# Two-block kernel: raw transposes of x with the norms applied at evacuation, and two reordered transitions

## The reference, cut to what matters

```python
h = concat([meta, x])                      # 1040 x 1024
u = rmsnorm(h, norm_g)                     # h * rsqrt(mean(h^2) + eps) * norm_g
f_in, f_gate, q, k, v, a_gate = split(u @ w_in)
f_out = (real(fftn(f_in, positions and channels)) @ w_fmix + b_fmix) * silu(f_gate)
a_out = gqa_attention(rope(rmsnorm(q)), rope(rmsnorm(k)), v) * silu(a_gate)
x = rmsnorm(h + concat([f_out, a_out]) @ w_out, final_g)[meta:]
# second block
p = rmsnorm(x, norm_mix_pre) @ w_in_2      # q, k, v, three convolution parts, two gates
merged = sigmoid(g_att) * (stick_breaking(q, k, v) @ w_att) + sigmoid(g_conv) * (conv(...) @ w_conv)
x = x + rmsnorm(merged @ w_out_2, norm_mix_post)
x = x + rmsnorm((gelu(conv(g)) * conv(a)) @ w_down, norm_ffn_post)   # g, a from rmsnorm(x, norm_ffn_pre) @ w_up
```

## Time and profile before

| What | Value |
|---|---|
| Median of 3 runs | 2228.54 us (2226.97 to 2229.95) |
| Profiled execution | 2228.94 us, span of its profile 2227.1 us |
| Mean granted TensorE clock | 0.981 of full speed |
| TensorE matmuls, share of the span | 2118.0 us, 95% |
| VectorE | 1115.5 us, 50% |
| ScalarE | 838.9 us, 38% |
| POOL | 745.9 us, 33% |

### The profile page before, as it was taken

How to read it: one execution, slowest core, us unless ns; L and a number is a source line. 1 busy time by engine, 2 the same in 40 slices (tenths; PEclk the granted TensorE clock), 3 DMA queues, 4 the chain that set the end, 5 groups by cost and what they waited for, 6 DMA issues and landing times.

```text
span 2227.1 us, 27859 instructions
## 1 busy us (share of the span) xinstructions
PE 2118.0 (95%) x10545; PEld 1747.8 (78%) x10545; DVE 1115.5 (50%) x1608; ACT 838.9 (38%) x1485; POOL 745.9 (33%) x661
## 2 busy tenths in 40 slices
PE   5899999999988999999999999989999999999996
PEld 4687888999767788787877888868888888878785
DVE  7347658888253376767657652442222222221523
ACT  5133228999232364554546421331221222111212
POOL 3222142222331322222222343233333333367672
PEclk7999999999999999999999999999999999999998
DMA  5031120010241211111212543421111111132432
GB/s 172 24 122 52 52 95 30 11 49 11 67 134 57 65 62 51 54 59 52 70 48 80 170 139 108 132 76 48 47 47 47 47 47 47 48 112 94 148 107 76
DMA packets 142923, 164.69 MB, mean 74 GB/s; under 512 B 7091, under 2 KB 108999, under 8 KB 142823
## 3 DMA queue, kind: packets, MB, share of 16 engines
q1 hardware_dynamic: 118663, 98.10, 14.4%
q10 hardware_dynamic: 24160, 65.23, 8.4%
HBM read 133.94 MB, written 29.36 MB: 73 GB/s over the span
## 4 chain that ended last, share of the span: by engine, by line
PE 84%; DVE 9%; ACT 3%; issue 2%; DMA 1%; ACTq 0%; POOL 0%; DVEq 0%
PE psum L667 18%; PE psum L669 18%; PE psum L668 18%; PE psum L989 15%; PE psum L885 3%; PE psum L897 3%; PE psum L1026 1%; PE psum L916 1%; PE psum L917 1%; PE psum L918 1%; DVE softplus_part L2146 1%; PE psum L1010 1%; PE psum L1011 1%; DVE xn L1847 1%; PE psum L1043 1%
## 5 line engine op out<-in xcount | busy, mean ns | idle before, releaser
L559 POOL TENSOR_TENSOR w_ring<-w_staging,zero 128x8 fp32r<-128x8 f32 x172 | 45.3, 263 | 1220.4 <-PE psum L669 748.6
L562 POOL TENSOR_TENSOR w_ring<-w_staging,w_ring 128x1024 fp32r<-128x1024 f32 (+1 forms) x172 | 444.1, 2582 | 14.4
L989 PE MATMUL psum<-h,w_ring 128*128 128x512 f32 x1728 | 434.6, 402 | 0.7 <-ACT v L1522 0.7
L989 PEld LDWEIGHTS psum<-h,w_ring 128*128 128x128 f32 x1728 | 317.8, 190 | 68.1 <-ACT v L1522 1.1
L667 PE MATMUL psum<-ffn_in,w_ring 128*128 128x512 f32 x672 | 265.4, 395 | 0.0
L669 PE MATMUL psum<-ffn_in,w_ring 128*128 128x512 f32 x672 | 264.3, 393 | 0.0
L668 PE MATMUL psum<-ffn_in,w_ring 128*128 128x512 f32 x672 | 263.8, 393 | 0.0
L2279 DVE SCALAR_TENSOR_TENSOR up_buf<-psum,vectors,up_buf 128x1023 f32<-128x1023 f32 x44 | 56.4, 1283 | 308.3 <-ACT up_buf L1743 308.3
L560 POOL TENSOR_SCALAR w_ring<-w_staging 128x1016 fp32r<-128x1016 f32 (+1 forms) x172 | 182.9, 1064 | 0.0
L1743 ACT ACTIVATE up_buf<-psum,vectors 128x1024 f32<-128x1024 f32 x44 | 49.2, 1117 | 268.0 <-PE psum L669 267.9
L669 PEld LDWEIGHTS psum<-ffn_in,w_ring 128*128 128x128 f32 x672 | 126.0, 188 | 30.4
(11 more groups left out here) (285 smaller groups left out, 4570.2 us busy)
## 6 DMA issues: line engine op xcount, KB each, us to landing
w_staging<-in_w_in SPq DMA_DIRECT2D x58, 512.0 KB, 3.8
w_staging<-in_w_up SPq DMA_DIRECT2D x44, 512.0 KB, 3.8
w_staging<-in_w_down SPq DMA_DIRECT2D x44, 512.0 KB, 3.2
w_staging<-in_w_out SPq DMA_DIRECT2D x16, 512.0 KB, 3.8
scratch_gates<-gate_out ACTq DMA_DIRECT2D x32, 256.0 KB, 2.4
merge_gates<-scratch_gates ACTq DMA_DIRECT2D x16, 512.0 KB, 4.5
x_again<-scratch_x ACTq DMA_DIRECT2D x16, 512.0 KB, 4.4
xin<-in_x ACTq DMA_DIRECT2D x8, 512.0 KB, 3.2
```

The lines of the kernel that those rows point to most:

```text
L562: pool.tensor_tensor(lo[:, 0:width], WS[:, s, 0:width], plain(hi[:, 0:width]), ALU.subtract).then_inc(S["w_split"], 1)
L989: ins = pe.matmul(mix_bank(h), (sl if x == 2 else sh)[:, P * k:P * k + P], ml if x == 1 else mh, start=m == 0, stop=m == UNIT // 2 - 1)
```

## The change

*Head.* TensorE transposes the raw tiles of x, the meta tile first, into three PSUM buffers, without waiting for a norm. For each group (the meta tile, then pairs) VectorE refines the inverse norms; TensorE turns them too, as columns broadcast to 128 wide, into bank 6 or 7, so that every partition holds the row of inverse norms; VectorE copies that row to `RB` and multiplies it into the transposed tile as it empties PSUM into `UT`. ScalarE no longer empties these tiles. The gain norm_g is per feature, which is now per partition: it comes in as rows of the small vector table (two more small loads on SP) and is applied as scalar operand in the two halves of the fold. The full gain for the later second normalisation loads last in ScalarE's queue. The identity is first in SP's queue. POOL's first splits wait until all inverse norms are refined (`nt_xn` at 9).

*First transition.* Behind the output projection's second half only tiles 0 to 3 are transposed, tiles 4 to 7 go behind units 0 to 3 of V2. VectorE makes the low half of a tile one turn later. ScalarE copies V2's units 0 to 2 in the last three turns of its loop.

*Second transition.* In a turn ScalarE makes the high half ahead of the second square, and VectorE the low half ahead of refine.

```diff
...
+FIRST = [(TT,)] + [(t, t + 1) for t in range(0, TT, 2)]
+FIRST_TILES = [t for group in FIRST for t in group]
...
+        def first_gain(k):
+
+            row = 2 * FT + 4 + k % 4
+            return VEC[:, 1 + k // 4, row:row + 1]
...
+            for x in range(2):
+                sp.dma_start(VROW[nf + 4:nf + 8, 1 + x, :],
+                             a["norm_g"][0, FW * x:FW * x + FW].rearrange("(m d) -> m d", d=P)).then_inc(S["vec_in"], 16)
...
+            sp.dma_start(IDENT[:, :], const["ident"]).then_inc(S["consts"], 16)
             for t in range(1, KTILES, 2):
                 sp.dma_start(XALL[0:tokens_of(t)[1], t, :], x_tile(t)).then_inc(S[f"x_in{t}"], 16)
-                if t == 1:
-                    sp.dma_start(IDENT[:, :], const["ident"]).then_inc(S["consts"], 16)
...
+            pool.wait_ge(S["nt_xn"], KTILES)
             for c in range(peeled):
...
-            pe.wait_ge(S["consts"], 16 * N_CONSTS)
-
-            for t in range(KTILES):
-                transpose_tile(N_U + t, N_U, N_U, tokens_of(t)[1])
-
-            pe.wait_ge(S["vec_in"], 48)
+            pe.wait_ge(S["consts"], 16)
+
+            for i, group in enumerate(FIRST):
+                rows = tokens_of(group[0])[1]
+                for t in group:
+                    n = FIRST_TILES.index(t)
+                    pe.wait_ge(S[f"x_in{t}"], 16)
+                    if n >= 3:
+                        pe.wait_ge(S["nt_free"], n - 2)
+                    for k in range(KT):
+                        ins = pe.transpose(pair_tiles(n % 3)[:, k, 0:rows], XALL[0:rows, t, P * k:P * k + P], IDENT[0:rows, 0:rows])
+                    ins.then_inc(S["nt_mm"], 1)
+                pe.wait_ge(S["nt_xn"], n + 1)
+                if i >= 2:
+                    pe.wait_ge(S["nt_free"], 2 * i - 3)
+                for x, t in enumerate(group):
+                    ins = pe.transpose(PB[:, 6 + i % 2, P * x:P * x + rows], RX[0:rows, t:t + 1].broadcast_to([rows, P]),
+                                       IDENT[0:rows, 0:rows])
+                ins.then_inc(S["rb_mm"], 1)
+            pe.wait_ge(S["nt_free"], KTILES - 2)
+
+            pe.wait_ge(S["vec_in"], 80)
...
-                     after=lambda u: transpose_tile(N_A2 + u - LAG, N_A2, N_A2) if u >= LAG else None)
+                     after=lambda u: transpose_tile(N_A2 + u - LAG, N_A2, N_A2) if LAG <= u < TT - 1 else None)
...
-                     after=lambda u: transpose_tile(N_A2 + TT - LAG + u, N_A2, N_A2) if u < LAG else None)
+                     after=lambda u: transpose_tile(N_A2 + TT - 1 - LAG + u, N_A2, N_A2) if u <= LAG else None)
...
-            for t in range(0, KTILES, 2):
+            for t in (TT, 0, 2, 4, 6):
                 act.dma_start(XALL[0:tokens_of(t)[1], t, :], x_tile(t)).then_inc(S[f"x_in{t}"], 16)
                 if t == 0:
-                    act.dma_start(GB[N_U][:, :], a["norm_g"][0, :].partition_broadcast(P)).then_inc(S["consts"], 16)
                     load_tables()
+            act.dma_start(GB[N_U][:, :], a["norm_g"][0, :].partition_broadcast(P)).then_inc(S["gain_in"], 16)
...
-            for t in range(0, KTILES, 2):
-                both = range(t, min(t + 2, KTILES))
-                for x in both:
-                    rows = tokens_of(x)[1]
+            for group in FIRST:
+                rows = tokens_of(group[0])[1]
+                for x in group:
                     act.wait_ge(S[f"x_in{x}"], 16)
                     link(act.activation(JUNK0[0:rows, :], XALL[0:rows, x, :], ACT.Square, accum_out=SS[0:rows, x:x + 1]))
-                guess(rows, t, len(both), 1.0 / D, False)
-                if t:
-                    u_out(t - 2)
-                    u_out(t - 1)
-            u_out(KTILES - 1)
+                guess(rows, group[0], len(group), 1.0 / D, False)
...
-                act.activation(AF[:, 0, k, FOLDS * h:FOLDS * h + n], FSUM[:, j % 2, 0:n], ACT.Copy).then_inc(S["fold_hi"], 1)
+                act.activation(AF[:, 0, k, FOLDS * h:FOLDS * h + n], FSUM[:, j % 2, 0:n], ACT.Copy,
+                               scale=first_gain(k)).then_inc(S["fold_hi"], 1)
...
+                if s >= TT:
+                    value_copy(s - TT)
...
-            for u in range(TT):
-                n = T_V2 + u
-                ready(n)
-                act.activation(VR[:, u, :], PB[:, tm_bank(n), :], ACT.Copy).then_inc(S["tm_free"], 1)
+            for u in range(LAG, TT):
+                value_copy(u)
...
+                if s >= LAG:
+                    hi_of_tile(N_A4 + s - LAG, A4, s - LAG)
                 if 1 <= s <= TT:
...
                 guess_pair(s)
-                if s >= LAG:
-                    hi_of_tile(N_A4 + s - LAG, A4, s - LAG)
...
+            v.wait_ge(S["consts"], 16)
+            for i, group in enumerate(FIRST):
+                rows = tokens_of(group[0])[1]
+                refine(rows, group[0], len(group), 1.0 / D, RX)
+                v.sem_inc(S["nt_xn"], len(group))
+                v.wait_ge(S["rb_mm"], i + 1)
+                w = P * (len(group) - 1) + rows
+                link(v.tensor_copy(RB[:, i % 2, 0:w], PB[:, 6 + i % 2, 0:w]))
+                for x, t in enumerate(group):
+                    n = FIRST_TILES.index(t)
+                    first = tokens_of(t)[0]
+                    v.wait_ge(S["nt_mm"], n + 1)
+                    v.tensor_tensor(UT[:, :, first:first + rows], pair_tiles(n % 3)[:, :, 0:rows],
+                                    RB[:, i % 2, P * x:P * x + rows].unsqueeze(1).broadcast_to([P, KT, rows]),
+                                    ALU.mult).then_inc(S["nt_free"], 1)
...
-            for s in range(TT + LAG):
+            for s in range(TT + LAG + 1):
                 if s < TT:
                     residual(TT + s)
...
-                if s >= LAG:
-                    lo_of_tile(N_A2 + s - LAG, A2, P * (s - LAG))
+                if s > LAG:
+                    lo_of_tile(N_A2 + s - LAG - 1, A2, P * (s - LAG - 1))
                 refine_pair(s)
...
             for s in range(TT + LAG):
+                if s >= LAG:
+                    lo_of_tile(N_A4 + s - LAG, A4, P * (s - LAG))
                 refine_pair(s)
...
                     normalise(N_A4, t, Y[:, t, :], RX[:, 8 + t:9 + t])
-                if s >= LAG:
-                    lo_of_tile(N_A4 + s - LAG, A4, P * (s - LAG))
...
```

More of the change, by code:

```diff
@@ L237 @@
 x_in0 x_in1 x_in2 x_in3 x_in4 x_in5 x_in6 x_in7 x_in8
-zero_set w_staged0 w_staged1 w_hi w_split w_used tm_mm tm_free fm_free nt_in0 nt_in1 nt_xn nt_mm nt_hi nt_free
+zero_set w_staged0 w_staged1 w_hi w_split w_used tm_mm tm_free fm_free nt_in0 nt_in1 nt_xn nt_mm nt_hi nt_free rb_mm gain_in
 v_chain a_chain rs_ss rs_y consts vec_zero vec_in vec_t vec_done rope_in cw_zero cw_in cw_mm cw_hi cw_done
@@ L303, in two_block_kernel @@
         XALL = at("x_tiles", [P, KTILES, D], R1)
+        RB = at("rstd_rows", [P, 2, 2 * P], R2 + 12288)
         JUNK0 = at("junk0", [P, D], R1 + KTILES * D)
@@ L1253, in _ @@
                 n = FOLD + 1 - 2 * h
+                if j == 0:
+                    act.wait_ge(S["vec_done"], 1)
                 act.wait_ge(S["fold_sum"], j + 1)
-                act.activation(AF[:, 0, k, FOLDS * h:FOLDS * h + n], FSUM[:, j % 2, 0:n], ACT.Copy).then_inc(S["fold_hi"], 1)
+                act.activation(AF[:, 0, k, FOLDS * h:FOLDS * h + n], FSUM[:, j % 2, 0:n], ACT.Copy,
+                               scale=first_gain(k)).then_inc(S["fold_hi"], 1)
             act.wait_ge(S["cw_mm"], 1)
@@ L1498, in hi_of_tile, with value_copy @@
                 act.activation(dst[:, 0, :, P * t:P * t + P], pair_tiles(n % 2), ACT.Copy).then_inc(S["nt_hi"], 1)
+            def value_copy(u):
+                ready(T_V2 + u)
+                act.activation(VR[:, u, :], PB[:, tm_bank(T_V2 + u), :], ACT.Copy).then_inc(S["tm_free"], 1)
             load_tables()
@@ L1856, in _ @@
             v.memset(WBD[:, :, :], 0.0).then_inc(S["cw_zero"], 1)
-            v.wait_ge(S["consts"], 16 * N_CONSTS)
-            for t in range(KTILES):
-                rows = tokens_of(t)[1]
-                if t % 2 == 0:
-                    n = min(2, KTILES - t)
-                    refine(rows, t, n, 1.0 / D, RX)
-                normalise(N_U, t, XALL[0:rows, t, :], RX[0:rows, t:t + 1], rows)
+            v.wait_ge(S["consts"], 16)
[13 more added lines that the diff above has]
+                                    ALU.mult).then_inc(S["nt_free"], 1)
             v.wait_ge(S["vec_t"], 1)
@@ L1875, in fold_lo @@
                 v.wait_ge(S["fold_hi"], j + 1)
-                v.tensor_tensor(AF[:, 1, k, FOLDS * h:FOLDS * h + n], FSUM[:, j % 2, 0:n],
-                                plain(AF[:, 0, k, FOLDS * h:FOLDS * h + n]), ALU.subtract).then_inc(S["fold_done"], 1)
+                v.scalar_tensor_tensor(out=AF[:, 1, k, FOLDS * h:FOLDS * h + n], in0=FSUM[:, j % 2, 0:n], scalar=first_gain(k),
+                                       in1=plain(AF[:, 0, k, FOLDS * h:FOLDS * h + n]), op0=ALU.mult,
```

(2 more changed lines are left out.)

## The result

The changed kernel takes 2213.63 us in the median of four executions (2212.58 to 2214.38), the kernel before 2229.24 us beside it (2226.97 to 2231.94): a ratio of 0.9929, with a 95% interval of 0.9912 to 0.9946. That is 15.6 us less, where 17.8 were summed, and the time lies inside the range of 2202 to 2217. The profiled execution took 2214.38 us with a span of 2212.6. In the runs further down one execution, the sixth of e11, took 3473.05 us at a granted clock of 0.556, and it is left out of e11's figures.

What follows compares the result with a forecast made beforehand. TensorE, carrying 84% of the chain of waits, was taken as the bound. Head 2.6, first transition 9.6 and second 5.6 sum to 17.8 us off 2228.5, giving 2210.7; predicted time 2210.5 us, range 2202 to 2217.

Steps and rivals of the forecast that it cites:

- Head, 2.6 forecast: Head: fold starts at 26.0 instead of 38.94 but POOL's splits stretch it; its end moves from 62.1 to 59.5, gaining 2.6 us.
- The scalar operands of the fold's two halves leave their lengths as they are: Head: applying the gain as scalar operand was to add no time to the fold, own length 23.2 us.
- 59.5 - 26.0 - 23.2 = 10.3: Head: fold end 59.5, less start 26.0, less own length 23.2, leaves the time POOL's splits add.
- The column copies, which I left half open: Head: eight 0.16 us copies inside the fold may run beside POOL (end 58.9) or wait (end 60.2); 59.5 taken.
- First transition, 9.6 forecast: Output projection to V2: 9.0 us up to tile 4's transposition, plus the 0.57 us wait of tile 6.
- The rival in which the clock falls in that wait: First transition: V2's unit 0 waits for POOL's fourth split, ready at 672, clock drops; gain 6.5 us, time 2213.8; chance 0.10.
- Second transition, 5.6 forecast: Second output projection to up projection: last low half ready at 1470.5 against 1476.06, a gain of 5.6 us.
- TensorE starts at 1452.65: Second transition: after tile 3's high half (1.00) and low half (1.22), TensorE starts at 1452.65, not 1458.00.
- The lower bound, 4: Second transition: the gain would be 4 us if the copies collide on ScalarE; the upper bound was 6.5.
- head gives nothing: Rival: port collision holds VectorE's products too, or small loads come late; fold ends at 64.7, time 2215.9; chance 0.15.
- head gives its whole start: Rival: POOL finds gaps, fold ends at 49 to 52; gain 10 to 12.9 us, time near 2201; chance 0.10.
- slower: Rival: locked fold instructions each wait out POOL and more, fold ends after 82; time 2233 or more; chance 0.02.

Runs made afterwards that it cites:

- e11: The changed kernel with no edit, timed again on one chip beside e12; 2212.31 us, 0.9925 of the kernel before.
- e4: The whole change run once more for a second profile; a single execution of 2214.74 us.
- e6: The changed kernel with POOL's first splits held until all sixteen folds are done; 2222.34 us, 0.9981 of the kernel before.
- e2: The kernel before with only the first transition changed; 0.9968 of the kernel before.
- e7: The changed kernel with tile 4 transposed inside V2's unit 0, after its second chunk; 2212.20 us, 0.9930 of the kernel before.
- e10: The changed kernel with POOL's early splits and ScalarE's last copy of the second output projection moved ahead; 2207.58 us, 0.9916 of the kernel before.
- e5: The changed kernel without POOL's wait for the norms, so its first splits start when the weights land; 2208.00 us, 0.9922 of the kernel before.
- e9: The changed kernel with the edits of e5 and e7, and ScalarE's last output projection copy moved ahead; 2209.54 us, 0.9927 of the kernel before.
- e12: The changed kernel with the same two edits as e10, on the same chip as e11; 2207.02 us, 0.9911 of the kernel before.

## Why the prediction was right, and where its sizes were off

**Head, 2.6 forecast, 3.66 measured in the first profile.** It is 2.94 and 3.28 in e4 and e11, and 3.2 from the mean resumption of six profiles with the new head (67.03) and three with the old (70.19). The mechanism was right. The fold began at 25.10, not 26.0; POOL at 21.76, not 22.2; the fold took 33.3 us, not 33.5; TensorE resumed 8.11 us behind its end, as said. So most of the difference is the earlier start, 0.9 us. That the length of the fold came out so well is luck: inside the 33.3 us two terms are off and cancel. "The scalar operands of the fold's two halves leave their lengths as they are" is wrong: two low halves take 1.64 us where they took 1.49, and 16 times 0.075 is 1.2; the fold by itself is 24.3 us (e6) and not 23.2. And POOL adds 33.3 - 24.3 = 9.0 us, not the 59.5 - 26.0 - 23.2 = 10.3 of the forecast: three low halves at 2.85 to 2.90 in place of 0.75 add 6.4, four column copies at 0.36 to 1.05 in place of 0.17 add 2.8, and the sums stay at 0.70 (there POOL's subtraction waits, 2.92 us for 2.39), where I had nearly all of POOL's time added to the fold. The column copies, which I left half open, do wait: 1.00 to 1.05 us beside POOL against 0.17, as long as the POOL row of 1.03 us that begins with them. The Trainium skill, "SBUF — State Buffer", Who interferes with whom, had this as the second half of its rule, that copies within SBUF in a two-port mode want the shared ports; the trace agrees that they wait, with 1.05 against 0.17 us, and no run shows the mode itself. The products from PSUM were free, as forecast: 1.22 us in 23.74 to 24.96, inside a POOL subtraction from 23.04 to 25.43.

**First transition, 9.6 forecast, 9.4 measured where the clock held.** Tile 2 waited 0.43 us (0.4 forecast). V2's unit 0 waits for POOL and no longer for xn, but twice, 1.74 and 1.93 us in place of one wait of 2.9: POOL's splits took 652.25 to 669.55, 17.3 us, where I took 16.5 from the earlier trace rows, and the third was late as well. The rival in which the clock falls in that wait is what e4 and e2 show (7.4 and 7.7 us, forecast 6.5): it is no other course of the change but happens in some of its executions, in five profiles of eleven (with e6, e7 and e10).

**Second transition, 5.6 forecast, 4.3 measured.** Here two steps failed. The first is "TensorE starts at 1452.65". I named the low half as what ends the wait, because the row of before names it, and did not ask which PSUM bank the half unit writes. The reorder puts ScalarE's last copy behind high half, second square and guess, and TensorE waits 2.34 us where I had 1.45. That by itself cost nothing against the sum: 5.92 us came in e5 and e6, where the clock held. The second is the clock, which the sum had as held in the shorter pause. It fell behind the 2.34 us in five profiles of seven, to 0.57 to 0.75 over the next 3 us, and took 1.6 us. The lower bound, 4, was near, for a reason that I only half named ("the copies collide on ScalarE").

**The sum.** 17.3 us in the three places against 17.8, and 15.6 in the medians, with an interval from 12.0 to 19.6 (0.54% to 0.88% of 2229.24) that holds both. In part this is luck: in the first profile the head gave 1.1 us more than forecast and the second transition 1.3 less, and the 3.2 us that the clock took elsewhere were in no term. The rivals "head gives nothing", "head gives its whole start" and "slower" fell: the fold ended at 58.44, not at 64.7, 49 or 82.

## What to carry to other kernels

Before reordering an engine's queue, list for the waiting instruction every semaphore that it needs, the PSUM bank that it overwrites among them: the profile names only one, and moving that one earlier shows the next (here a copy of 0.58 us on ScalarE). Put work of POOL beside VectorE's rows that read PSUM, not beside rows that read SBUF twice or copy within it: e5 did this by deleting one wait and TensorE resumed 2.6 us earlier. And place an effect by comparing event times of the two traces, stage by stage, in more than one profile, since the clock behind a single pause moves a whole execution by about 1.5 to 3.5 us.

## What the runs showed that I had not expected

Pauses of TensorE as short as 1.44 us (336 to 338), and of 2.3 to 2.6 us, are followed by the lower clock in one execution and not in another of the same length and surroundings: 0.50 and 1.00 in e9 and e12 behind 2.37 us. The falls that can be sized here cost about 1.5 to 3.5 us each. The spread between executions goes loosely with the mean clock: among those of the kernel before beside e11, the three at 0.981 took 2228.87 to 2230.80 us and the three at 0.984 took 2225.51 to 2226.80, with the five between them from 2226.30 to 2230.13; e10's five go from 2204.63 us at 0.989 to 2211.64 at 0.984. At the second transition the pause of 1.56 us in place of 2.34 brought 0.3 us by itself, and a fall there costs 1.6. No fall in four profiles against five falls in seven are few; if it holds, most of what that pause costs is the clock. That the shorter pause prevents the fall is not shown.
